# One head's high and low values side by side as the stationary operand, and the two halves of the product added on ScalarE and VectorE

## What is computed

```python
def mla_attention(q_nope, q_rope, k_nope, k_rope, v):
    scale = (MLA_NOPE_DIM + MLA_ROPE_DIM) ** -0.5
...
        s = (jnp.einsum('bqhd,bkhd->bhqk', qn, k_nope).astype(jnp.float32)
             + jnp.einsum('bqhr,bkr->bhqk', qr, k_rope).astype(jnp.float32))
        p = jax.nn.softmax(s * scale, axis=-1).astype(v.dtype)
        return jnp.einsum('bhqk,bkhd->bqhd', p, v)
...
    o_mla = mla_attention(q_nope, q_rope, k_nope, k_rope, v_mla).reshape(b, s, MLA_WIDTH)
```

## Time and profile before

| | before |
|---|---|
| median of 3 runs | 807.73 us (806.52 to 808.02) |
| the profiled execution | 805.57 us |
| its span, first to last instruction | 803.8 us |
| mean granted TensorE clock | 0.965 of 2.4 GHz |
| busy: TensorE matmuls, weight loads | 731.7 us (91%), 605.2 us (75%) |
| busy: VectorE, ScalarE, GpSimd | 584.3 us (73%), 482.3 us (60%), 266.3 us (33%) |

### The profile page before, as it was taken

The page is one execution under the profiler, slowest core; times in us unless marked ns, Lnnn a source line. Parts: engine busy times, 40 slices in busy tenths (PEclk is TensorE's granted clock), DMA queues, the critical chain, the costliest instruction groups (busy, mean ns, idle before and its releaser), DMA issues. The chain is left out here.

```text
span 803.8 us, 12631 instructions
## 1 busy us (share of the span) xinstructions
PE 731.7 (91%) x3799; PEld 605.2 (75%) x3799; DVE 584.3 (73%) x975; ACT 482.3 (60%) x874; POOL 266.3 (33%) x292
## 2 busy tenths in 40 slices
PE   3999989998899789999998299999999999999985
PEld 3898878777778577777788277888887777777862
DVE  6974355545554676777676879999989888888857
ACT  3334345445554565666135447888878778888735
POOL 3133256554655243334421114222322222222111
PEclk9999999999999969999997599999999999999998
DMA  9724320222025593122734749999999999999863
GB/s 344 252 90 139 110 79 2 80 66 66 1 66 181 182 342 109 35 94 79 261 137 186 272 145 361 390 375 388 397 388 374 379 373 368 389 378 376 303 212 157
DMA packets 71484, 179.35 MB, mean 223 GB/s; under 512 B 11687, under 2 KB 28071, under 8 KB 71444
## 3 DMA queue, kind: packets, MB, share of 16 engines
q1 hardware_dynamic: 66692, 166.34, 54.8%
q0 software_dynamic: 4752, 12.51, 6.3%
HBM read 153.20 MB, written 30.42 MB: 228 GB/s over the span
## 5 line engine op out<-in xcount | busy, mean ns | idle before, releaser
L2325 DVE TENSOR_TENSOR eDl<-rawD,eDh 128x1024 fp32r<-128x1024 f32 x68 | 80.3, 1222 | 12.3 <-ACT eDh L2254 12.1
L1266 POOL TENSOR_SCALAR me<-me,mrec 128x512 f32<-128x512 f32 (+1 forms) x48 | 64.9, 1355 | 55.4 <-DVE mrec L1445 55.4
L2325 DVE TENSOR_TENSOR eUl<-rawU,eUh 128x1024 fp32r<-128x1024 f32 x68 | 78.8, 1221 | 4.2 <-ACT eUh L2254 2.5
L2325 DVE TENSOR_TENSOR eGl<-rawG,eGh 128x1024 fp32r<-128x1024 f32 x64 | 75.4, 1223 | 6.8 <-ACT eGh L2254 6.2
L2449 POOL DMA_INDIRECT acc_rows<-yg,idx_s x16 | 29.7, 1858 | 134.5 <-ACT yg L2279 134.5
L2254 ACT ACTIVATE eGh<-rawG 128x1024 fp32r<-128x1024 f32 x64 | 65.5, 1058 | 7.0 <-DMA rawG<-in_w_gate 5.3
L1072 ACT ACTIVATE pT_h<-bank 128x512 fp32r<-128x512 f32 (+1 forms) x48 | 25.3, 526 | 73.8 <-PE bank L782 73.8
L1451 DVE TENSOR_TENSOR pT_l<-bank,pT_h 128x512 fp32r<-128x512 f32 (+1 forms) x48 | 28.9, 602 | 50.2 <-ACT pT_h L1072 50.2
L2254 ACT ACTIVATE eDh<-rawD 128x1024 fp32r<-128x1024 f32 x64 | 64.0, 1056 | 0.0
L2168 PE MATMUL bank<-eGh,xgT_h 128*128 128x512 f32 x136 | 56.6, 417 | 7.8 <-DVE xgT_l L2330 6.7
L2254 ACT ACTIVATE eUh<-rawU 128x1024 fp32r<-128x1024 f32 x64 | 62.8, 1051 | 0.0
(11 more groups left out here) (343 smaller groups left out, 2156.4 us busy)
## 6 DMA issues: line engine op xcount, KB each, us to landing
rawG<-in_w_gate SPq DMA_DIRECT2D x68, 512.0 KB, 15.2
rawU<-in_w_up SPq DMA_DIRECT2D x68, 512.0 KB, 12.1
rawD<-in_w_down SPq DMA_DIRECT2D x68, 512.0 KB, 13.4
wb_raw<-in_w_in SPq DMA_DIRECT2D x8, 512.0 KB, 4.6
wo_raw<-in_w_o SPq DMA_DIRECT2D x8, 512.0 KB, 7.7
xln_rows<-res SPq DMA_DIRECT2D x6, 512.0 KB, 3.8
dqk_high<-st_h SPq DMA_DIRECT2D x8, 384.0 KB, 2.3
dqk_low<-st_l SPq DMA_DIRECT2D x8, 384.0 KB, 3.3
```

The source lines that it names most:

```text
L1266: nc.gpsimd.tensor_scalar(e, e, mrec[:, g % NSB:g % NSB + 1], None, ALU.mult).then_inc(m_p, 1)
L2325: nc.vector.tensor_tensor(wl_[X][i][:], raw_of(X, t, i)[:], f32(wh_[X][i][:]), ALU.subtract).then_inc(s_lo[X], 1)
```

## The change

Per head the high and the low values now lie side by side in one tile (`v_hl`, 64 columns each), and this is the stationary operand. One matmul with the high probabilities and one with the low ones give, per key tile, the high values' product in one half of the rows and the low values' in the other: two matmuls for three. (The product of low by low, which was left out, is now part of the sum.) The two halves have to be added: ScalarE copies the half that lies in the other head's rows to the rows of this head (`mix_moved`, to `mixM_sum` in SBUF), VectorE adds the other half from PSUM (`mix_summed`), and ScalarE and VectorE then make the high and low parts from the sum in SBUF. Bank 6 is free after the sum. In slots 0 and 2 ScalarE's order is now `probs_high`, `mix_moved`, `exp`, `mix_high`; VectorE does the sum where it did `mix_low`, and `mix_low` one slot later, in slots 1 and 3; for the last two units `mix_low` follows the sum at once.

```diff
@@ the products (TensorE)
-                wait(pe, m_ml, w)
-            vs = slice((h % 4) // 2 * P, (h % 4) // 2 * P + P)
-            pairs = three([(v_h[h // 4][:, t, vs], v_l[h // 4][:, t, vs], pT_h[x][:, j, :], pT_l[x][:, j, :])
-                           for j, t in enumerate(range(SEQS[x][0] // P, SEQS[x][0] // P + nk))])
-
-            last = products(psum[6][:, 0:n], pairs, 3 * js[0], 3 * js[-1] + 3)
+                wait(pe, m_ml, 2 * w - 1)
+            pairs = []
+            for j, t in enumerate(range(SEQS[x][0] // P, SEQS[x][0] // P + nk)):
+                v = v_hl[h // 4][:, t, h % 4, :]
+                pairs += [(v, pT_h[x][:, j, :]), (v, pT_l[x][:, j, :])]
+
+            last = products(psum[6][:, 0:n], pairs, 2 * js[0], 2 * js[-1] + 2)
...
             if g < 2:
-                pe.wait_ge(m_ml, 2 * HEADS)
+                pe.wait_ge(m_ml, 4 * HEADS)
@@ ScalarE
+        def mix_moved(w):
+            h, x = w // 2, w % 2
+            t0, n, _ = SEQS[x]
+            r, other = (slice(VDIM * i, VDIM * i + VDIM) for i in (h % 2, 1 - h % 2))
+            act.wait_ge(m_pv, w + 1)
+            nc.scalar.activation(mixM_sum[h // 2][r, t0:t0 + n], psum[6][other, 0:n], ACT.Copy).then_inc(m_mh, 1)
+
         def mix_high(w):
             h, x = w // 2, w % 2
             t0, n, _ = SEQS[x]
             r = slice(VDIM * (h % 2), VDIM * (h % 2) + VDIM)
-            act.wait_ge(m_pv, w + 1)
-            nc.scalar.activation(mixM_h[r, h // 2, t0:t0 + n], psum[6][r, 0:n], ACT.Copy).then_inc(m_mh, 1)
+            act.wait_ge(m_ml, 2 * w + 1)
+            nc.scalar.activation(mixM_h[h // 2][r, t0:t0 + n], mixM_sum[h // 2][r, t0:t0 + n], ACT.Copy).then_inc(m_mh, 1)
...
-            if i == 0 and h:
-                mix_high(2 * h - 2)
-            if i == 2 and h:
-                mix_high(2 * h - 1)
+            w = {0: 2 * h - 2, 2: 2 * h - 1}.get(i, -1)
+            if w >= 0:
+                mix_moved(w)
             if s + 3 < MT:
                 exp(s + 3)
+            if w >= 0:
+                mix_high(w)
@@ VectorE
+        def mix_summed(w):
+            h, x = w // 2, w % 2
+            t0, n, _ = SEQS[x]
+            r = slice(VDIM * (h % 2), VDIM * (h % 2) + VDIM)
+            total = mixM_sum[h // 2][r, t0:t0 + n]
+            dve.wait_ge(m_mh, 2 * w + 1)
+            nc.vector.tensor_tensor(total, total, psum[6][r, 0:n], ALU.add).then_inc(m_ml, 1)
+
         def mix_low(w):
...
-            dve.wait_ge(m_mh, w + 1)
-            nc.vector.tensor_tensor(mixM_l[r, h // 2, t0:t0 + n], psum[6][r, 0:n], f32(mixM_h[r, h // 2, t0:t0 + n]),
-                                    ALU.subtract).then_inc(m_ml, 1)
+            dve.wait_ge(m_mh, 2 * w + 2)
+            nc.vector.tensor_tensor(mixM_l[h // 2][r, t0:t0 + n], mixM_sum[h // 2][r, t0:t0 + n],
+                                    f32(mixM_h[h // 2][r, t0:t0 + n]), ALU.subtract).then_inc(m_ml, 1)
...
-            if i == 0 and h:
-                mix_low(2 * h - 2)
-            if i == 2 and h:
-                mix_low(2 * h - 1)
+            w = {0: 2 * h - 2, 2: 2 * h - 1}.get(i, -1)
+            if w >= 0:
+                mix_summed(w)
+                if s >= MT:
+                    mix_low(w)
+            if s < MT and i in (1, 3) and h:
+                mix_low(2 * h - 2 + i // 2)
```

More of the change, by code:

```diff
@@ L149, in encoder_trunk @@
     st_l = at("st_l", 121, [P, TOK], FR)
-    v_h = [at(f"v_h{i}", (132, 18)[i], [P, NT, 4 * VDIM], FR) for i in range(2)]
-    v_l = [at(f"v_l{i}", (144, 24)[i], [P, NT, 4 * VDIM], FR) for i in range(2)]
+    v_hl = [at(f"v_hl{i}", (138, 18)[i], [P, NT, 4, 2 * VDIM], FR) for i in range(2)]
     pT_h = [at(f"pT_h{x}", 178 + 16 * x, [P, SEQS[x][2], SEQS[x][1]], FR) for x in range(2)]
@@ L155, in encoder_trunk @@
     me = [at(f"me{i}", 198 + 2 * i, [P, 512]) for i in range(NME)]
-    mixM_h = at("mixM_h", 126, [P, HEADS // 2, TOK], FR)
-    mixM_l = at("mixM_l", 138, [P, HEADS // 2, TOK], FR)
+    mixM_h = [at(f"mixM_h{c}", 126 + 12 * (c // 2) + 3 * (c % 2), [P, TOK], FR) for c in range(HEADS // 2)]
+    mixM_sum = [at(f"mixM_sum{c}", 132 + 12 * (c // 2) + 3 * (c % 2), [P, TOK]) for c in range(HEADS // 2)]
+    mixM_l = [at(f"mixM_l{c}", 132 + 12 * (c // 2) + 3 * (c % 2), [P, TOK], FR) for c in range(HEADS // 2)]
     mixD_h = at("mixD_h", 162, [P, DH, TOK], FR)
@@ L332, in filled @@
             vs = slice(2 * g[2], 2 * g[2] + 2)
-            return bank[:].rearrange("p (t n) -> p t n", t=2), v_h[g[1]][:, vs, :], v_l[g[1]][:, vs, :]
+            v = v_hl[g[1]][:, vs, :, :]
+            return bank[:].rearrange("p (t h n) -> p t h n", t=2, h=4), v[:, :, :, 0:VDIM], v[:, :, :, VDIM:2 * VDIM]
         t0, n, _ = SEQS[g[2]]
@@ L510, in mix_parts @@
     def mix_parts(n, c):
-        return ((mixM_h, mixM_l), (mixD_h, mixD_l))[n][0][:, c, :], ((mixM_h, mixM_l), (mixD_h, mixD_l))[n][1][:, c, :]
+        return (mixM_h[c][:], mixM_l[c][:]) if n == 0 else (mixD_h[:, c, :], mixD_l[:, c, :])
     def front_sync(sp):
@@ L880, in o_part @@
                 if n == 0:
-                    pe.wait_ge(m_ml, 2 * HEADS if t >= NT_P else 2 * HEADS - 1)
+                    pe.wait_ge(m_ml, 4 * HEADS if t >= NT_P else 4 * HEADS - 2)
                     pe.wait_ge(m_ptl, MT)
```

## The result

The changed kernel took 810.51 us (median of 22 runs, 808.49 to 816.82) against 807.75 us before (22 runs, 805.87 to 811.37). The ratio is 1.0037 with an interval of 1.0022 to 1.0051: some 3.0 us slower. The forecast was 806.0 us, with 802.0 to 809.5 for eight in ten. The sum of the prediction was -1.7 us; the kernel lost 3.

What follows compares the result with a forecast made beforehand. TensorE was taken to bound 112 to 268 us, short engine-to-engine chains 268 to 297 us. The terms -8.1 + 3.2 + 0.3 + 2.9 = -1.7 us gave 806.0 us from the median 807.73, range 802.0 to 809.5.

Steps and rivals of the forecast that it cites:

- first term: Products of heads 0 to 6, 112 to 268 us: removed matmuls save 1.16 us per head, 8.1 us in all.
- price of a matmul: TensorE's start-to-start time in a stream: 0.230 us for 512 columns, 0.118 us for 256.
- Slot 3: VectorE's `mix_low` ahead of the low part of "K": taken at 0, at most 1.7 us from `k_l` waits.
- `v_l` wait: Head 4, low part of the values behind `mix_low` on VectorE: 0.3 us more waiting, between 0 and 0.6.
- Slot 2: ScalarE's `mix_high` waits for VectorE's sum, delaying the "K" product 0.8 us in heads 1, 2, 3, 5: 3.2 us.
- step over: Passage to the second attention group, 268 to 297 us, VectorE's order is the path: 2.9 us later, from 1.3 to 4.
- copy across partitions: ScalarE's `mix_moved` from bank 6 costs what the copy in place does (0.37 and 0.59 us): nothing extra.
- rival of a double price: Copy to other partitions costs double, `q_raw` waits grow by 2 us: +0.3 us, 808.0, no change; chance 0.18.
- rival of half clock: Longer TensorE waits bring 1.2 GHz stretches, 1.4 us each; with three more, 810.1 us; chance 0.12.

Runs made afterwards that it cites:

- two products alone: Kernel before with only the products changed, two matmuls per key tile, no copy or sum, low values' product left out: 803.88 us, ratio 0.9936.
- three and one: Three key tiles in slot 4, one in slot 5, instead of two and two: 802.66 us on two products alone, 809.18 us on the changed kernel.
- all four orders: Changed kernel, "B" first in slot 2, key tiles three and one, `mix_low` last in slots 1, 3, last two units' `mix_low` later: 804.78, again 805.03 us.
- head 7 changed: Changed kernel with slots 2, 3, 4 reordered; head 7 has three products, no sum, step over in the order of before: 805.75 us, ratio 0.9973.
- new order in slot 2: Changed kernel with ScalarE making the high part of the "B" block before `mix_high` in slot 2: 809.64 us, ratio 1.0012 to before.
- version with the low part later: Changed kernel with the last two units' `mix_low` moved behind the second group's slot on VectorE: 811.79 us, ratio 1.0038 to before.

## Why the prediction was wrong

*The step that failed* is the first term: "For heads 0 to 6, whose products lie in the stretch that TensorE bounds, 7 x 1.16 = 8.1 us". The price of a matmul was right (0.21 for 0.230), and so was the bound of the stretch as a whole. But the prediction's own condition, "a matmul less is time gained unless something new holds TensorE", was examined for every step that the change adds and not for the slots from which it takes work. In slot 4 the removed matmuls were the cover of the chain `k_h`, `k_l`, bank 5. In head 2 slot 4 lasted 3.80 us before and 3.77 after. That took 1.9 of the 8.1 us by the five waits, shown from both sides: present with two products alone (a gain of 5.7), gone with three and one (7.4; in the changed kernel three and one gave 2.3).

*Slot 3* was taken at nothing, and two new waits on `k_l` of 0.26 and 0.23 us came. They are not `mix_low` standing ahead of the low part of "K", for they stay when it is moved; their cause is open.

*The `v_l` wait* was priced at 0.3 and measured 1.0 (1.58 to 2.58): a mis-sized term, above the range given for it (0 to 0.6). Of the 1.0, 0.2 is there with two products alone (1.82), and 0.6 goes when `mix_low` is moved.

*Slot 2* held: 3.2 priced, 4.0 - 1.0 = 3.0 us of new waits in heads 1, 2, 3 and 5; undoing it gave 2.2.

*The step over* held to the tenth: 2.9 priced, 2.9 measured. At the first bias step, ahead of the last two units, 0.6 of it is there (272.57, 5.54 us after "B", for 4.94 before; 0.7 priced), and 1.4 and 0.9 are in units 14 and 15 (1.3 and 0.9 priced).

*The copy across partitions* costs nothing, as taken. The groups of the changed kernel, 112 to 290 us:

```profile
L1082 ACT ACTIVATE mixM_sum<-bank 64x512 f32<-64x512 f32 x8 | 4.7, 593 | 0.2
L1089 ACT ACTIVATE mixM_h<-mixM_sum 64x512 fp32r<-64x512 f32 x8 | 5.0, 630 | 0.9 <-DVE mixM_sum L1470 0.8
L1477 DVE TENSOR_TENSOR mixM_l<-mixM_sum,mixM_h 64x512 fp32r<-64x512 f32 x8 | 5.5, 692 | 0.8 <-ACT mixM_h L1089 0.7
```

593 ns, against 0.59 us for the copy in place; the rival of a double price falls.

*So without the pieces up to "B"* the sum is: stretch -1.5, step over +2.9, that is +1.4 us where -1.7 was forecast. The 3.1 between are the 1.9 of slot 4, the 0.5 of slot 3 and the 0.7 of `v_l`; the rest (0.2 less in slot 2, 0.2 that I can't place) cancels. The measured loss is 3.0, so some 1.6 us are left.

*What comes after.* The prediction let what is won or lost before 297 us pass to the end in full. From the first output product to the end it is 517.3 us before, and 518.3 and 518.5 in the two profiles of the changed kernel: about 1 us more is lost there, and no run shows by what. The versions that came to that product sooner than before took longer behind it (520.7 in both with two products alone, 518.6 and 523.4 with all four orders, 523.1 with head 7 changed), so a gain did not pass in full either, as far as single profiles tell.

*The clock.* The mean clock of the changed kernel's runs is 0.9597, that of before 0.9622; at 0.66 us for 0.001 (the line through the runs of before) that would be 1.6 us, just what is left. But the clock can't be set, and this estimate may count the same time twice. Here are the stretches around the step over, before, after and in the second profile of the changed kernel:

```profile
265.00:310.00 45.00, 37.17 (x206) 29.04 (x207) 30.65 (x79) 26.66 (x73) 13.45 (x17) 0.81 0.65 234
...
265.00:310.00 45.00, 33.15 (x182) 25.64 (x181) 30.56 (x76) 26.98 (x71) 13.50 (x18) 0.77 0.64 234
...
265.00:310.00 45.00, 33.10 (x178) 25.39 (x178) 29.65 (x75) 26.02 (x69) 13.47 (x17) 0.77 0.64 234
```

The lower clock there is worth 0.04 x 45 = 1.8 us, or 0.0022 of the 0.0025 between the means, and part of it falls ahead of the first output product, in time that the 2.9 us hold already. The second profile has no more pieces up to "B" than before, and its span (807.1 us) is still 3.3 us longer: 0.4 up to the first turned tile, -1.3 from there to "B", +2.9 in the step over, +1.3 after it. So a loss of 3 us needs no further piece up to "B"; how much the clock adds to it stays open. By the runs at 0.965 alone (four of the changed kernel at 808.7, 23 of before at 806.3) the part at equal clock is 2.4, by the lines at 0.960 1.5. The rival of half clock foresaw 1.4 us for a stretch, and one measures 1.7. Its 810.1 us came near by luck: it wanted three such stretches more and no failed term; up to "B" one profile has one more, the other none. The changed kernel's two new ones in the first profile:

```profile
115.00:120.00 5.00, 3.20 (x10) 2.72 (x11) 2.51 (x7) 2.24 (x7) 4.18 (x4) 0.68 0.71 225
205.00:210.00 5.00, 4.09 (x12) 3.30 (x13) 2.33 (x7) 1.38 (x5) 1.38 (x2) 0.66 0.00 0
```

Before, both had 1.00, and the one near 190 us is missing after. The one at 205 follows the wait on `v_hl`: it is in seven of the nine profiles in which that wait was 1.97 us or longer and in none of the three with 1.58 to 1.82. That is a coincidence in time, not a cause shown. The place near 117 follows a wait of 2.1 us on GpSimd that is in all profiles, before's too, while the low clock is in five of twelve. The Trainium skill (TensorE: Matmul & The Clock Gate, section Part 1) has the array throttled by default and released by activity; the trace agrees in so far as all three places follow a wait of about 2 us, but such a wait was not always followed by it.

## What to carry to other kernels

When a change removes work from an in-order engine, look slot by slot at what ended just under that work: a chain that lands 0.03 us after the cover ends is in the trace of before, stands in no list of waits there, and takes the whole gain of that slot. Then ask where else the remaining work may lie; moving one key tile gave back some 2 us, as much as the new order in slot 2. A step that goes from one engine to another and back belongs behind what others wait for in both queues, and moving it later helps only if the next step of the same chain does not then stand behind it.

## What the runs showed of the hardware

VectorE's `mix_low` from SBUF took 692 ns on average, no less than the 684 ns from PSUM. In the step over, where it had been moved, it took 1.15 us beside a GpSimd instruction of 1.66 us; the timeline of the version with the low part later:

```profile
284.75 1.15 DVE L1477 TENSOR_TENSOR mixM_l<-mixM_sum,mixM_h 64x512 fp32r<-64x512 f32 x1
...
283.70 1.66 POOL L1297 TENSOR_SCALAR ee<-ee,erec,lam_col 128x512 f32<-128x512 f32 x1 [4.46 <-DVE erec L1529]
```

The Trainium skill (SBUF — State Buffer, section SBUF: two separate sides) says that a VectorE instruction with two SBUF inputs and a GpSimd one that reads SBUF block each other; this row goes that way. In the changed kernel at 204.35 us, beside a GpSimd instruction all along, it took only 0.78, which a full block does not explain, and at 271.26 us, for 256 columns and also beside one all along, 0.41 us, no more than without (0.41 at 145.76). What made the row of 1.15 us slow is not shown.

The matmuls with the same values in a row (`pT_h`, then `pT_l`) were not cheaper for it: their starts stand 0.23 us apart as before (215.11 and 215.34 in head 4), and every one has its own weight load (0.19 us in the timeline), as the busy times of the changed kernel's page count them:

```profile
PE 725.2 (90%) x3751; PEld 598.9 (74%) x3751; DVE 592.1 (73%) x991; ACT 492.7 (61%) x890; POOL 266.5 (33%) x292
```
